# Fewer low parts ahead of three reciprocal roots, token sums one feature earlier, and vector 6's rows loaded and copied earlier, in a fused two-block kernel on one core

## The reference, cut to what matters

```
c_act = silu(c)
mod = (c_act @ w_ada + b_ada).reshape(b, 3, 3, 1024)        # vectors 0..8
h = rms_norm(x) * (1 + mod[:, 0, 1]) + mod[:, 0, 0]         # ffn 0
x = x + 0.5 * mod[:, 0, 2] * swiglu(h, ffn_w13[0], ffn_w2[0])
h = rms_norm(x) * (1 + mod[:, 1, 1]) + mod[:, 1, 0]         # mixer 1
q, kv, conv_in, gate_logits = split(h @ w_in)               # 8 heads, a 3-tap convolution, 2 x 1024 gates
branches = stack([causal_attention(q, kv), gate_b * conv(gate_c * xv)])
y = sum_g(sigmoid(gates[g]) * (branches[g] @ w_branch[g])) @ w_out
x = x + mod[:, 1, 2] * y
h = rms_norm(x) * (1 + mod[:, 2, 1]) + mod[:, 2, 0]         # ffn 1: root A, vectors 6, 7, 8
x = x + 0.5 * mod[:, 2, 2] * swiglu(h, ffn_w13[1], ffn_w2[1])
# second block
z = rmsnorm(x) @ w_in_2                                     # root B
x = x + (gate_a * mixer_a(z) @ w_out_a + gate_b * mixer_b(z) @ w_out_b) @ w_out_2
x = x + square(relu(rmsnorm(x) @ w_ff1)) @ w_ff2            # root C
x = x + sigmoid(rmsnorm(x) @ w_ple_gate) * (p @ w_ple)
return rmsnorm(x)
```

## Time and profile before

| | before |
|---|---|
| median of three runs | 1035.67 us (1032.38 to 1036.63) |
| profiled execution: own time | 1032.17 us |
| its span | 1030.3 us |
| PE busy | 1003.8 us, 97% |
| DVE busy | 716.9 us, 70% |
| ACT busy | 537.9 us, 52% |
| POOL busy | 36.2 us, 4% |
| mean granted clock of PE | 0.995 |

### The profile page before, as it was taken

One profiled execution on the slowest core, in us unless ns is written; L12 is line 12 of the kernel. 1 busy time (PEld: TensorE's weight loads), 2 busy tenths in 40 slices (PEclk: granted clock), 3 DMA queues, 4 the chain that ended last, 5 costly groups with the idle time before them and its releaser, 6 DMA issues.

```text
span 1030.3 us, 19345 instructions
## 1 busy us (share of the span) xinstructions
PE 1003.8 (97%) x8248; PEld 976.5 (95%) x8248; DVE 716.9 (70%) x1234; ACT 537.9 (52%) x903; POOL 36.2 (4%) x71
## 2 busy tenths in 40 slices
PE   8999999999999998999999989999999899999997
PEld 6999999999999988999999869999999899999997
DVE  3587888878787888667656759656566865555586
ACT  4455443556666456444444658555465545444553
POOL 0111000000000010000000000004000000000000
PEclk9999999999999999999999999999999999999999
DMA  9989979957455774577655356436258565556521
GB/s 337 365 258 361 314 281 332 331 170 244 136 166 183 255 235 164 204 247 234 216 169 200 113 174 191 137 123 184 68 180 267 173 193 176 183 186 199 170 83 42
DMA packets 140382, 212.24 MB, mean 206 GB/s; under 512 B 4275, under 2 KB 114215, under 8 KB 140296
## 3 DMA queue, kind: packets, MB, share of 16 engines
q1 hardware_dynamic: 135936, 198.66, 57.4%
q0 software_dynamic: 4096, 12.10, 3.9%
q10 hardware_dynamic: 264, 0.25, 0.1%
HBM read 209.88 MB, written 1.11 MB: 205 GB/s over the span
## 4 chain that ended last, share of the span: by engine, by line
PE 87%; DVE 9%; ACT 2%; DMA 2%; issue 1%; SPq 0%; DVEq 0%
PE PS L472 85%; DVE wlo L1853 5%; PE PS L480 2%; DMA SC<-in_w_ada_dram 1%; DVE W L1795 1%; DVE W L1804 1%; ACT whi L1338 1%; DVE SS L1795 1%; DVE sm L1804 1%; DMA SC<-in_x_dram 0%; DVE hl L1804 0%; ACT W L1325 0%; DVE sm L1798 0%; DVE SR L1795 0%; DVE xT L1804 0%
## 5 line engine op out<-in xcount | busy, mean ns | idle before, releaser
L1853 DVE TENSOR_TENSOR wlo<-raw,whi 128x1024 fp32r<-128x1024 f32 (+2 forms) x331 | 386.4, 1186 | 155.7 <-ACT whi L1338 155.1
L1338 ACT ACTIVATE whi<-raw 128x1024 fp32r<-128x1024 f32 (+2 forms) x331 | 333.0, 1025 | 171.5 <-PE PS L472 147.8
L472 PE MATMUL PS<-hh,wlo 128*128 128x256 f32 (+1 forms) x1376 | 386.4, 282 | 0.0
L472 PE MATMUL PS<-hl,whi 128*128 128x256 f32 (+1 forms) x1376 | 385.7, 282 | 0.0
L472 PE MATMUL PS<-hh,whi 128*128 128x256 f32 (+1 forms) x1376 | 385.0, 286 | 0.0
L472 PE MATMUL PS<-SR,whi 128*128 128x256 f32 (+1 forms) x1824 | 327.8, 282 | 0.3 <-DVE SR L1795 0.3
L472 PEld LDWEIGHTS PS<-SR,whi 128*128 128x128 f32 x1824 | 280.0, 188 | 1.7 <-issue 1.7
L472 PEld LDWEIGHTS PS<-hl,whi 128*128 128x128 f32 x1376 | 261.0, 190 | 0.4
L472 PEld LDWEIGHTS PS<-hh,wlo 128*128 128x128 f32 x1376 | 260.7, 189 | 0.0
L472 PEld LDWEIGHTS PS<-hh,whi 128*128 128x128 f32 x1376 | 256.7, 189 | 3.1 <-issue 2.2
L472 PE MATMUL PS<-SR,wlo 128*128 128x256 f32 (+1 forms) x912 | 256.9, 282 | 0.0
(11 more groups left out here) (190 smaller groups left out, 746.7 us busy)
## 6 DMA issues: line engine op xcount, KB each, us to landing
raw<-in_ffn_w_dram SPq DMA_DIRECT2D x60, 1024.0 KB, 6.9
raw<-in_w_in_dram SPq DMA_DIRECT2D x37, 1024.0 KB, 5.4
raw<-in_w_ff_dram SPq DMA_DIRECT2D x32, 1024.0 KB, 5.5
raw<-in_w_ada_dram SPq DMA_DIRECT2D x20, 1024.0 KB, 5.5
SC<-in_w_ada_dram SPq DMA_DIRECT2D x8, 1024.0 KB, 10.6
SC<-in_w_ada_dram POOLq DMA_DIRECT2D x8, 1024.0 KB, 7.2
raw<-in_w_out_dram SPq DMA_DIRECT2D x8, 1024.0 KB, 5.0
raw<-in_ffn_w_dram SPq DMA_DIRECT2D x7, 768.0 KB, 10.0
```

The lines of the kernel that those rows point to most:

```text
L472: return e.matmul(o, l, r, start=start, stop=stop, skip_group_check=True)
L1338: e.activation(hi_part(p), raw_part(p), ACT.Copy).then_inc(*hi_done.up(p.i))
L1853: e.tensor_tensor(lo_part(p), raw_part(p), hi32(hi_part(p)), ALU.subtract).then_inc(*lo_done.up(p.i))
```

## The change

Five edits. Ahead of the roots, DVE makes at most one further low part at A and C and none beyond what PE needs at B, instead of all that ACT has copied. The token sums of A and C are written ahead of the last feature of the `mm_low` loop. Vector 6's loads go behind `gate` 5, 6 and 7 and behind the first `out1`, instead of between the branch loads. In round 3 of the heads loop DVE makes one low part instead of two. ACT copies vector 6's rows out ahead of stage 6 instead of stage 7.

```diff
@@ lay_out @@
         for i in range(5, 8):
             self.tall("gate", w_in, GATE0 + 256 * i)
+            self.ada(w_ada, 6, i - 5)
         wb = a["w_branch"][0].rearrange("g k d -> (g k) d")
         self.tall("branch", wb, 0)
-        self.ada(w_ada, 6, 0)
         for j in range(2, 8, 2):
             self.tall("branch", wb, 128 * j)
-            if j < 6:
-                self.ada(w_ada, 6, j // 2 + j // 4)
             self.row("out1", a["w_out"][0], j - 2)
             if j == 2:
-                self.ada(w_ada, 6, 2)
+                self.ada(w_ada, 6, 3)
@@ pe_program, root A (root C alike, with gm 3,7 and token_sums(7, 3)) @@
             for k in range(KD):
+                if k == 7:
+                    on.wait_ge(dve_done, ("x", 1, 4))
+                    token_sums(0, 1)
                 on.wait_ge(dve_done, (("xs1", 1), k))
...
-            on.wait_ge(dve_done, ("x", 1, 4))
-            token_sums(0, 1)
@@ act_program, gated @@
-                    if j == 7 and last:
+                    if j == 6 and last:
                         last()
@@ dve_program, heads loop @@
-                    lo_for(round1(i - 1), 2 if i < HEADS + 1 else HEADS + 2 - i)
+                    lo_for(round1(i - 1), 1 if i == 3 else 2 if i < HEADS + 1 else HEADS + 2 - i)
@@ dve_program, roots A, B, C @@
-            lo_for(("sums", 1))
+            lo_for(("sums", 1), 1)
-            lo_for(("by_pair", 0))
+            lo_for(("by_pair", 0), 0)
-            lo_for(("sums", 3))
+            lo_for(("sums", 3), 1)
```

More of the change, by code:

```diff
@@ L1136, in pe_program @@
             for k in range(KD):
+                if k == 7:
+                    on.wait_ge(dve_done, ("gm", 3, 7))
+                    token_sums(7, 3)
                 on.wait_ge(dve_done, (("xs1", 3), k))
@@ L1141, in pe_program @@
                         m.then_inc(*count(("used", p.i), ("f", i // 2, i % 2)))
-            on.wait_ge(dve_done, ("gm", 3, 7))
-            token_sums(7, 3)
             relu_tile(1, 1)
```

## The result

| | before | after |
|---|---|---|
| median | 1036.04 us (1032.38 to 1036.63) | 1018.19 us (1017.48 to 1020.27) |
| ratio to before | | 0.9838 (0.9811 to 0.9865) |
| profiled execution: own time, span | 1032.17, 1030.3 us | 1018.01, 1016.2 us |

The change made the kernel 17.9 us faster in the medians and 14.2 in the profiled executions. 1019.5 was forecast, from a sum of 14.3.

A forecast was written before the change was run, and what follows sets the result against it. TensorE, 97% busy, was held by waits and low clock. 2.9 - 2.26 - 3.23 - 4.07 - 1.7 - 4.53 - 1.7 + 0.1 + 0.2 = -14.3 us, giving 1017.9 or 1021.4; forecast 1019.5 us, range 1014 to 1027.

The forecast's parts named there:

- A: Root behind the mixer, first `rstd_row` matmuls at 400.97 us: TensorE's 3.23 us wait for `sm` goes whole.
- C: Root ahead of ff1, at 818.76 us: the 4.53 us wait for `sm` goes, plus 1.7 us of clock.
- B: Root where the second block begins, at 597.01 us: the 4.07 us wait for `sm` goes, plus 1.7 us of clock.
- The three roots: At A, B and C: waits for `sm` of 3.23, 4.07 and 4.53 us go, plus 1.7 us of clock at B and C each.
- The new wait in the heads loop: TensorE's three transposes near 319 us: 2.9 us of wait, as row sums delay DVE's `SC<-SC,PS`; bounds 0 and 4.6.
- Its clock: Clock behind the new wait in the heads loop: claimed to stay up, nothing charged.
- rival two: Heads loop: the new wait stretches to 4.6 us, costing 1.7 us more and 1.7 of clock: 1023 us; chance 0.17.
- The HT step: Turn of vector 6, 376.77 us: 2.26 us wait goes, with ACT's copy at least 1.3 us earlier and TensorE 2.9 later.
- The loads: Vector 6's loads ahead of `gate` 6, `gate` 7 and `branch` in a four-slot ring: priced at 0, range 0 to 1 us.
- Low parts come due: Low parts put behind the roots may come late for TensorE: 0.2 us at A, 0 at B, 0.1 at C.
- rival three: Behind the roots: a third of the fourteen deferred low parts delays TensorE, 5.7 us back: 1025 us; chance 0.17.
- the two bases: Forecast gain of 14.3 us taken from the profiled execution's 1032.17 us (1017.9) or the median's 1035.67 us (1021.4).

The follow-up runs named there:

- sums_only: The kernel before with only the two token sums of A and C moved ahead of the last feature, without the limits: 1024.99 us.
- conv_first: The changed kernel with DVE's `SC<-SC,PS` of round 5 put ahead of that round's row sums and low part: 1014.79 us, run again 1014.62 us.
- ht_back: The changed kernel with ACT's copy of vector 6's rows taken back to stage 7: 1019.87 us in one run.
- sums_in_place: The changed kernel with the two token sums back behind the loop and the limits kept: 1021.4 us.
- roots_only: The kernel before with only the three limits at the roots and the moved token sums: 1016.47 us.
- loop_only: The kernel before with only vector 6's loads moved, the limit in round 3 and ACT's copy at stage 6: 1035.36 us.
- roots_bc: The kernel before with roots B and C changed (limits, and C's token sums) and root A as before: 1022.19 us.

## Why the prediction was right, step by step

*The three roots* held as steps and sizes. All three waits went whole, and the clock of B and C stayed at 1.00: 3.5, 4.4, 6.3 and 1.8 us in the table against 3.2, 3.9, 6.2 and 1.6. One credit was given wrongly: at A and C most of the low parts' move comes with the token sums and not with the limits, as `sums_only` shows.

*The new wait in the heads loop* came at the place, by the chain and with the size that were worked out: 2.9 forecast, 3.19 printed. The copy ended at 322.19, as worked out; TensorE had been idle since 322.34 - 3.19 = 319.15, and started 0.15 after the copy's end. `conv_first` shows the chain by removing it.

*Its clock* is the step that failed: "It is shorter than the 3.23 behind which the clock stayed at 1.00, so I charge nothing for the clock." That row was one execution of something that varies. Five profiled executions with the heads loop's wait at 2.2 to 3.2 us had a mean clock of 0.50 or 0.66 behind it, every time; A's wait had 1.00, 0.70 and 0.50. Three of the five windows stand above; the other two, of `ht_back` and `sums_in_place`, behind waits of 3.03 and 3.18 us:

```profile
322.60:327.60 5.00, 4.97 (x21) 3.78 (x22) 3.18 (x11) 2.79 (x9) 0.00 (x0) 0.50 0.81 278
...
322.80:327.80 5.00, 5.00 (x21) 3.78 (x22) 3.18 (x11) 2.79 (x9) 0.00 (x0) 0.50 0.80 283
```

So rival two's second half came true without its first: 1.7 us. The Trainium skill, "TensorE: Matmul & The Clock Gate", section "HAM oscillation — how this bites in real kernels", describes waits that put the array back to its lower clock again and again. The gaps that it warns of are longer than these five waits and than A's 3.23, so that A's 1.00 does not speak against it; that the clock fell behind 2.19 to 3.20 us goes beyond it, and here the measurement decides.

*The HT step* went as forecast, but for one of its two reasons: TensorE's lateness, as `ht_back` shows. *The loads* cost nothing on the path, as priced, although ACT did wait for `gate` 6. *Low parts come due*: rival three did not occur in the changed kernel; `sums_in_place` shows that without the moved sums 1.33 us of it come at C.

That the sum of 14.3 matched the profiled 14.2 to a tenth is luck: two errors of about 1.1 us cancelled. The uncharged clock made the second row of the table 1.1 us worse (1.6 by the starts, less a wait of 0.33 for DVE's `SR` at 350.73 that only the kernel before has, and 0.2 that was not followed to rows), and the four rows below it came out 0.1 to 0.5 better each. In the medians the gain was 17.9. The forecast went between the two bases, 1017.9 and 1021.4; the measured 1018.19 lies at the profiled one. The likely reason, argued and not shown, is that the trace of before lacks losses of clock behind A and behind the turn of vector 6 that others of its executions have, and that the changed kernel has no wait at either place to lose them at. For it: its mean clock is 0.995, where twelve of the 17 executions of before beside `roots_only` have 0.992 or less.

## What to carry to other kernels

A limit on one engine's background work has to be read together with the place where the other engine's program counts: here the key that moved by one feature changed more than the limit itself. Background work moved to an earlier stage belongs behind whatever another engine's queue waits for in that stage; row sums that cost 3.2 us of wait and 1.7 of clock ahead of one `SC<-SC,PS` cost nothing seen in a gap 9 us later. And a removed wait is worth what stands behind it: 2.2 us at the turn of vector 6 were worth 0.7 at most in the medians, since the next tile was 1.1 late.

## What the runs showed of the hardware

The clock behind a wait of one length at one place differs from execution to execution. Over 5 us it was 1.00, 0.70 and 0.50 behind 3.22 to 3.23 us at root A (the kernel before, `loop_only`, `roots_bc`). It was 1.00 twice and 0.66 twice behind 2.24 to 2.26 us ahead of the turn of vector 6: 1.00 in the kernel before and in `roots_only`, 0.66 in `roots_bc` (above) and in `sums_only`. The windows of `roots_only` and `sums_only`:

```profile
376.00:381.00 5.00, 4.93 (x42) 4.94 (x43) 4.68 (x8) 3.05 (x6) 3.61 (x6) 1.00 1.03 256
...
376.60:381.60 5.00, 4.95 (x29) 4.95 (x30) 4.41 (x7) 2.65 (x5) 3.62 (x6) 0.66 1.04 249
```

In the heads loop it was 0.50 or 0.66 behind 2.19 to 3.20 us in all five executions that have such a wait. Behind single waits of 0.75 us (`conv_first`), 1.11 us (root C of `sums_only`) and 1.33 us (`sums_in_place`) it stayed at 1.00. What decides between them stays open. A loss of up to 2.5 us at one place that one profiled execution does not show can be part of the median.
